# Constant products in front of eight waits of TensorE, in a two-block mixer kernel

## What is computed

```python
z  = modulate(rmsnorm(x, norm1_g), sh1, sc1) @ w_in;  zc = (the same of ctx)   # q k v, r k v, loras
x  = x + g1 * (concat([windowed_gqa(q, k, v, kc, vc), rwkv(z, zc)]) @ w_out)
x  = x + g2 * ((silu(h @ ffn_w1) * (h @ ffn_w3)) @ ffn_w2)     # h: normed, modulated x
x  = rmsnorm(x, final_norm_g)
mem_n = rmsnorm(mem_2, mem_norm_g_2)
x  = x + concat([retention(rmsnorm(x)), memory(mem_n @ w_mem_kv[0])]) @ w_out_a
kv = rmsnorm(x) @ w_kv
x  = x + concat([dilated(rmsnorm(x), kv), memory(mem_n @ w_mem_kv[1])]) @ w_out_b
return rmsnorm(x, final_norm_g_2)
```

## Time and profile before

| | |
|---|---|
| runs | 3775.57, 3781.46, 3782.75 us; median 3781.46 |
| the profiled execution | 3780.9 us, of which the span is 3778.9 |
| mean granted TensorE clock over the span | 0.988 |
| busy share of the span | PE 97%, PEld 84%, DVE 52%, ACT 45%, POOL 38% |
| chain that ended last, by engine | PE 86%, DVE 7%, ACT 3%, DMA 2%, issue 1%, POOL 1% |

### The profile page before, as it was taken

How to read it: one execution, slowest core, us unless ns; L and a number is a source line. 1 busy time by engine, 2 the same in 40 slices (tenths; PEclk the granted TensorE clock), 3 DMA queues, 4 the chain that set the end, 5 groups by cost and what they waited for, 6 DMA issues and landing times.

```text
span 3778.9 us, 67462 instructions
## 1 busy us (share of the span) xinstructions
PE 3661.5 (97%) x28120; PEld 3181.4 (84%) x28120; DVE 1974.7 (52%) x2470; ACT 1691.2 (45%) x2217; POOL 1427.4 (38%) x703
## 2 busy tenths in 40 slices
PE   8999999999999999999999999999999999999998
PEld 5778888778777888888888888988888888888897
DVE  2258877667656785444456455435343334433343
ACT  3442236655544443444454444444444444444443
POOL 2332223111123554544533454544444434343443
PEclk9999999999999999999999999999999999999999
DMA  9876874000034677565545555555655555555554
GB/s 336 301 249 235 293 268 151 31 3 3 22 120 155 224 248 236 184 195 184 195 159 184 174 172 173 168 167 169 208 170 181 177 170 176 174 175 175 169 172 134
DMA packets 183502, 668.77 MB, mean 177 GB/s; under 512 B 20480, under 2 KB 20608, under 8 KB 182560
## 3 DMA queue, kind: packets, MB, share of 16 engines
q1 hardware_dynamic: 177408, 645.12, 51.8%
q10 hardware_dynamic: 4512, 15.14, 1.1%
q0 software_dynamic: 1280, 4.20, 0.3%
HBM read 655.98 MB, written 8.39 MB: 176 GB/s over the span
## 4 chain that ended last, share of the span: by engine, by line
PE 86%; DVE 7%; ACT 3%; DMA 2%; issue 1%; POOL 1%; ACTq 0%; SPq 0%; DVEq 0%; POOLq 0%
PE ps L1129 72%; DVE whl L2198 1%; PE ps L1380 1%; ACT whl L1646 1%; PE ps L1367 1%; PE ps L1634 1%; PE ps L1618 1%; PE ps L1272 1%; DMA raw<-in_mem 1%; PE ps L1076 1%; PE ps L1507 1%; PE ps L1054 1%; DVE raw L2282 1%; PE ps L1359 1%; ACT work L1646 1%
## 5 line engine op out<-in xcount | busy, mean ns | idle before, releaser
L1129 PE MATMUL ps<-halves,whl 128*128 128x256 f32 (+1 forms) x14752 | 2574.2, 335 | 40.5 <-POOL whl L2863 10.5
L1129 PEld LDWEIGHTS ps<-halves,whl 128*128 128x128 f32 x14752 | 2238.0, 190 | 341.2 <-issue 44.8
L2863 POOL TENSOR_TENSOR whl<-raw,whl 128x1024 fp32r<-128x1024 f32 x508 | 1268.8, 2499 | 1743.0 <-ACT whl L1646 1742.8
L1646 ACT ACTIVATE whl<-raw 128x1024 fp32r<-128x1024 f32 x1016 | 1055.5, 1053 | 929.5 <-PE ps L1129 651.1
L2198 DVE TENSOR_TENSOR whl<-raw,whl 128x1024 fp32r<-128x1024 f32 x508 | 822.3, 1619 | 1120.6 <-ACT whl L1646 1120.4
L1129 PE MATMUL ps<-whl,halves 128*128 128x256 f32 x2752 | 483.7, 334 | 1.7 <-POOL whl L2863 1.7
L1129 PEld LDWEIGHTS ps<-whl,halves 128*128 128x128 f32 x2752 | 416.6, 188 | 58.8 <-issue 5.6
L1646 ACT ACTIVATE work<-ps 128x512 f32<-128x512 f32 (+1 forms) x202 | 115.1, 574 | 305.7 <-PE ps L1129 260.6
L2282 DVE SCALAR_TENSOR_TENSOR raw<-raw,mix 128x1024 f32<-128x1024 f32 x128 | 232.8, 1847 | 5.9 <-DMA raw<-in_adaT 5.7
L2198 DVE TENSOR_TENSOR work<-work,ps 128x512 f32<-128x512 f32 x155 | 106.2, 685 | 110.2 <-ACT work L1646 109.0
L2860 POOL COPY XD<-X 64x256 f32<-64x256 f32 x80 | 39.7, 505 | 318.3 <-DVE X L2198 316.0
(11 more groups left out here) (277 smaller groups left out, 2425.1 us busy)
## 6 DMA issues: line engine op xcount, KB each, us to landing
raw<-in_ffn SPq DMA_DIRECT2D x264, 512.0 KB, 4.3
raw<-in_w_kv SPq DMA_DIRECT2D x192, 512.0 KB, 3.7
raw<-in_w_in_b SPq DMA_DIRECT2D x160, 512.0 KB, 3.8
raw<-in_adaT SPq DMA_DIRECT2D x128, 512.0 KB, 5.5
raw<-in_w_in_a SPq DMA_DIRECT2D x128, 512.0 KB, 3.8
raw<-in_ada SPq DMA_DIRECT2D x64, 512.0 KB, 5.8
raw<-in_mem SPq DMA_DIRECT2D x64, 512.0 KB, 6.2
raw<-in_w_out_a SPq DMA_DIRECT2D x48, 512.0 KB, 4.1
```

What stands on the lines that cost most here:

```text
L1129: p = self.e.matmul(o, x, y, start=bi not in begun, stop=final and kc == 3 and m == len(pairs) - 1, skip_group_check=True)
L1646: return self.e.activation(out, in_, func, **kw)
L2863: return self.e.tensor_tensor(out, a, b, op)
```

## The change

A new helper `constants(b, count)` writes `count` fp32 products of the identity with 256 constant columns into bank `b`; nobody reads them, and the next product into the bank starts afresh. `PACED` becomes a table of counts. In `products` the constants now stand behind the waits for the weight halves and before the wait for the activations. Counts: `mem0,0` 7, `w_k,0` 6, `ffn1,0` 8, `w_in_b,32` 8, and the four old ones keep 1. Three more places: 7 in bank 7 in the job `w_out_b,0` at row group 0; 8 in bank 6 between `scores(0)` and `scores(1)` of the attention; 3 in bank 5 before the wait of the last `add_squares` of r = 3 and of r = 6. That is 54 products in place of 4.

```diff
-PACED = (("ffn2", 0, 0), ("ffn2", 4, 0), ("ffn1", 8, 0), ("ffn1", 12, 0))
+PACED = {("ffn2", 0, 0): 1, ("ffn2", 4, 0): 1, ("ffn1", 8, 0): 1, ("ffn1", 12, 0): 1,
+         ("mem0", 0, 0): 7, ("w_k", 0, 0): 6, ("ffn1", 0, 0): 8, ("w_in_b", 32, 0): 8}
...
+    def constants(self, b, count):
+
+        for _ in range(count):
+            self.e.matmul(self.G(b)[:, 0:256], self.ident, self.cst("ident", 256), start=True, stop=True, skip_group_check=True)
+
     def products(self, t, job, outs, w, kg, begun, final):
         hi, lo = (v.rearrange("p (c n) -> p c n", c=4) for v in self.hi_lo(t))
         self.wait_ge("hi", t.n)
         self.wait_ge("lo_g" if t.n % 2 else "lo_v", t.n)
+        if not begun:
+            self.constants(job.banks[0], PACED.get(job.key, 0))
+        if job.key == ("w_out_b", 0, 0) and kg == 0:
+            self.constants(7, 7)
         for kc in range(4):
...
-                if kc == 0 and not begun and job.key in PACED:
-                    self.e.matmul(self.G(job.banks[bi])[:, 0:256], self.ident, self.cst("ident", 256), start=True, stop=True, skip_group_check=True)
...
         scores(0)
+        self.wait_ge(*self.leaves[6])
+        self.constants(6, 8)
         scores(1)
...
         if n == 0:
             self.bank(4, "root_s", r + (r == 4))
+        if n == 7 and r in (3, 6):
+            self.wait_ge(*self.leaves[5])
+            self.constants(5, 3)
         self.wait_ge("sq_s", (r, n))
```

## The result

The changed kernel took 3784.99 us (median of 20 runs, 3779.91 to 3798.01); the kernel before, beside it, 3780.29 (20 runs, 3774.65 to 3784.56). The ratio is 1.0019, 95% interval 1.0012 to 1.0026: 4.5 to 9.8 us more, 7.2 in the middle (the medians lie 4.7 apart). From here on, a difference with an interval in microseconds is the ratio's, times 3780.

A forecast was written before the change was run, and what follows sets the result against it. TensorE, busy 97% of the span, was taken as the bound. Terms +3.04 + 3.04 - 1.47 - 0.95 - 0.6 - 1.3 gave +1.8 us on the median 3781.46, so 3783; range 3775.5 to 3790.

The forecast's parts named there:

- two costs of 3.04 each: At mem0 and w_out_b, seven constants each miss the wait and add 3.04 us to TensorE's time.
- gains of 4.3: Filled waits at w_k, attention, ffn1 and w_in_b keep the clock up: -1.47, -0.95, -0.6 and -1.3 us.
- mem0, at 73 us: At mem0, seven constants stand behind the weight wait and are paid at full clock's price: +3.04 us, bounds 1.2 and 6.1.
- w_k: Six constants fit inside the wait; TensorE is busy throughout behind it, so the gain stays: -1.47 us, bounds 0 and -1.47.
- attention: Eight constants fit the wait; second scores run 0.95 us faster, then VectorE sets the pace: -0.95 us, bounds 0 and -3.27.
- ffn1: Constants fit around the last sum; ScalarE's high half and the norm's chunks come earlier: -0.6 us, bounds 0 and -2.99.
- w_in_b: Constants fit the waits and the next weight split, which hangs on TensorE, comes earlier: -1.3 us, bounds -0.5 and -2.93.
- w_out_b, 3rd tile: At w_out_b, row group 0 runs third, so seven constants miss the wait and nothing hides them: +3.04 us.
- rival B: Constants neither hold nor raise the clock: no gains, 3.04 at w_out_b, 6.1 at mem0, +9.1 us (3790.6); chance 0.09.
- its half of +6.1: Constants do not hold the clock at the filled waits, but mem0 costs only 3.04: +6.1 us, 3787.5; chance 0.05.
- that chain moves up by up to 1.64: At w_in_b, ScalarE's high half of the next weight split waits for TensorE and could start up to 1.64 us earlier.
- Rival A: All half-clock time returns at the four filled waits: -10.7 us, with +6.1 of cost -4.6, that is 3777; chance 0.16.

The follow-up runs named there:

- experiment 4: Experiment 3 plus seven constants at mem0 ahead of the wait for weight halves and eight ahead of w_out_b's first product: 3778.01 us, ratio to the kernel before 0.9996.
- experiment 9: The kernel before with one change, the seventh head's decay table transfer (awaited at 2378 us) issued earlier: 3777.49 us, ratio 0.9992.
- experiment 3: The changed kernel without the constants at mem0 and w_out_b, leaving those at w_k, attention, ffn1 and w_in_b: 3780.17 us, ratio to the kernel before 1.0001.
- experiment 8: Experiment 4 without the constants at mem0 and w_k: 3778.86 us, ratio to the kernel before 0.9995.
- experiment 5: The kernel before with only the seven constants at mem0 added, behind the wait for the weight halves: 3783.81 us, ratio 1.0011.
- experiment 1: The changed kernel without the seven constants at mem0: 3783.67 us, ratio to the kernel before 1.0004.
- experiment 2: The changed kernel without the seven constants at w_out_b's row group 0: 3784.36 us, ratio to the kernel before 1.0011.
- experiment 7: Experiment 3 with each constant product replaced by four transposes of the identity in transpose mode: 3778.74 us, ratio to the kernel before 0.9997.

## Why the prediction was right, and where it was off

The forecast was no change, for two costs of 3.04 each and gains of 4.3, together +1.8. Both costs came as forecast and about half of the gains, so the verdict stands on the right mechanism; that the time fell into the range is owed to the width of the range too, since +1.8 lies below the measured interval.

The moves by stage, in us, from fourteen traces (the places with constants against the same places without; in brackets the number of traces). They run between the markers at 275 and 309 us for w_k, 544 and 588 for the attention, 1199 and 1249 for ffn1, 2523 and 2599 for w_in_b:

```
stage             with constants        without               difference  forecast
mem0, at 73 us    +2.96 .. +3.78 (4)    -0.26 .. +1.74 (8)    +3.2        +3.04
w_k               -0.11 .. -0.08 (8)    -0.10 .. +1.42 (6)    -0.8        -1.47
attention         -1.34 .. -0.47 (10)   -0.50 ..  0.00 (4)    -0.6        -0.95
ffn1              -0.79 .. -0.65 (10)   -0.75 ..  0.00 (4)    -0.2        -0.6
w_in_b            -0.62 .. -0.53 (9)    -0.54 .. +0.05 (5)    -0.5        -1.3
w_out_b, 3rd tile +3.02 .. +3.03 (3)     0.00          (7)    +3.0        +3.04
sum                                                           +4.1        +1.8
```

**The costs: right in mechanism and size.** Both sets stand where the prediction put them, at +3.2 and +3.0 for 3.04 each; four times the set cost four times as much. The 108 constant instructions ran where the prediction said that they would, and nothing covered them.

**Constants hold the clock: right; rival B falls.** By the number alone B's +9.1, or its half of +6.1, would fit better than +1.8. The clock decides: all four waits that the constants fill are followed by 1.00, and so are all 41 filled waits of the fourteen traces (w_k, attention, ffn1, w_in_b, and w_out_b from experiment 4 on), while the clock fell behind 28 of the 29 that were left empty. At mem0, where B wanted the half clock's price, the 16 products behind the constants ran in 3.17 us.

**The gains: the terms that were too large, -2.0 in place of -4.3.** Against the profile of before alone, from which the terms were taken, the filled places give -0.1 at w_k, -0.9 in the attention, -0.7 at ffn1 and -0.6 at w_in_b: two terms were sized right, and those of w_k (-1.47) and w_in_b (-1.3) were not. At w_k the step that failed is "Behind it TensorE is busy 214.60 of 214.60 us, so the gain stays". TensorE was busy there because it came late: the slow stretch had used up the time in which it would have waited. The kernel of experiment 9, which has no constants at w_k, shows it: in its trace the clock stayed at 1.00 behind the same wait of 3.02 us, and

```profile
283.93 1.61 PE L1129 MATMUL ps<-halves,whl 128*128 128x512 f32 x6 [3.02 <-DVE halves L2205]
285.71 11.20 PE L1129 MATMUL ps<-halves,whl 128*128 128x512 f32 x48 [0.17 <-DVE halves L2205]
297.49 2.81 PE L1129 MATMUL ps<-halves,whl 128*128 128x512 f32 x11 [0.58 <-DVE halves L2205]
```

TensorE waits 0.17 and 0.58 for VectorE's chunks, just as with constants (0.17 and 0.56 above). VectorE's tenth set of halves ends 13.50 us after TensorE's first product in the traces of before and of experiments 3, 8 and 9 alike, whatever the clock: the chunks set the pace, and of 1.47 only 0.1 was there to be had against that profile of before.

At w_in_b "that chain moves up by up to 1.64" held for one split only: in the nine traces with constants the markers gain 1.7 at it, and 1.1 of that is lost again at the next; what holds that next split back was not followed up.

**What I took for one number is several.** A term was worked out as the half of one profile's slow stretch. The same wait, unfilled, is followed by a slow stretch of another length in another execution. Experiment 5, w_k and then w_in_b, the latter followed by full clock:

```profile
286.20:292.90 6.70, 5.99 (x14) 4.76 (x15) 5.98 (x13) 4.32 (x10) 0.82 (x2) 0.50 0.64 237
...
2532.20:2535.50 3.30, 3.01 (x10) 2.65 (x11) 3.30 (x8) 2.04 (x5) 1.77 (x2) 0.50 0.00 0
2535.60:2538.60 3.00, 3.00 (x20) 2.61 (x19) 0.81 (x2) 1.87 (x4) 2.71 (x2) 1.00 0.00 0
```

The 6.7 us at w_k, 5.99 of them with products, cost 1.35 more than in the profile of before (2.93 us there); the 3.3 us at w_in_b cost no more than a filled wait (-0.54 against -0.57). Over all traces without constants at w_k, no slow stretch goes with -0.1, a short one with 0 to +0.2, a long one with +1.2 to +1.4: the short one is nearly hidden by VectorE's chunks, the long one is not. So filling a wait takes out the bad draws, and the mean gain at w_k, 0.8, is larger than one comparison of two profiles tells (0.1), while at w_in_b it is smaller (0.5 against 0.6).

**Rival A falls.** TensorE's products got their time back (the rows of 1.00), the span did not: of 10.7 us some 2 came back by the markers, and the times of experiment 3 stand at -2.6 to +3.4. The Trainium skill ("TensorE: Matmul & The Clock Gate", Terms) prices a throttled stretch by its length times one minus the clock's share; here the traces agree for the products (two tiles in 6.01 us with the wait filled, in 8.65 without) and not for the end.

**What stays open.** The markers sum to +4.1; the times say +4.5 to +9.8, the medians 4.7. By the same table experiment 1 should stand at +1.0, experiment 2 at +1.2 and experiment 3 at -2.0; they stand at +1.5 (-1.9 to +4.9), +4.2 (+0.8 to +7.2) and +0.4 (-2.6 to +3.4), each within its interval and each above, so some of those 2 us may not be there at all. Runs that differ by 15 us among themselves don't settle 2.

## What to carry to other kernels

Put filler behind nothing that the engine waits for: it has to stand ahead of the wait that ends last, in program order, and at the tile that runs first in the schedule's own order; one wait or one tile too late and it is pure cost, count times price. It has to fit as well: in experiment 4 mem0's seven stood ahead of the wait, outlasted it by 2 us and gained nothing. Before counting a slow stretch as a gain, ask what the next operand's engine was doing: "busy 100%" at half clock can hide a producer that is only just late enough. And where effects of 1 to 3 us are at stake, compare a stage over several traces, since one profile of before is a single draw.

## What the hardware showed that I had not expected

- Transposes in transpose mode keep the granted clock at 1.00 across waits of 3 to 4 us (experiment 7).
- A wait of 3.02 us with nothing in it was followed by a clock of 1.00 in one execution (experiment 9), by 0.50 with 2.93 us of products in another and with 5.99 us in a third (experiment 5).
- From 2790 to 3600 us, where TensorE never waits and the clock is 1.00, the same products take 788.38 us in seven traces and 791.4 in seven others, nothing between. Experiments 4 and 3, the whole stretch, and its 512-column products (x count, busy us, mean ns):

```profile
2784.00:3572.38 788.38, 788.38 (x4687) 699.50 (x4686) 314.10 (x351) 342.05 (x411) 315.57 (x131) 1.00 0.56 175
...
L1137 PE MATMUL ps<-halves,whl 128*128 128x512 f32 x1461 | 509.8, 391 | 0.0
```

```profile
2779.77:3571.15 791.38, 791.38 (x4686) 699.91 (x4686) 313.92 (x351) 341.95 (x410) 315.52 (x131) 1.00 0.55 174
...
L1135 PE MATMUL ps<-halves,whl 128*128 128x512 f32 x1461 | 511.9, 393 | 0.0
```

  It is 3.0 us, as much as one of the terms of this case, and falls on kernels with and without the constants at w_in_b. What sets it was not found.
- A transfer 1 us late cost 4.8 us: VectorE came 0.10 us behind the next instruction of GpSimd, ended 1.1 us after it and so took 3.33 in place of 1.99 us, TensorE's wait grew from 1.74 to 4.03, and the clock fell behind it. In eight traces in which the transfer came less late, TensorE's wait did not change by more than 0.02 us.
